# VectorE takes a slot's score maximum ahead of the q and k norm work in forgetting attention

## What is computed

```
q, k, v, g, f_logit = split(x @ w_in)              # 16 heads of 64
qh, kh = rms_norm(heads(q), qn_g), rms_norm(heads(k), kn_g)
c = cumsum(log_sigmoid(f_logit + b_f))             # per head, over time
s = (qh @ kh.T) / sqrt(64) + (c[t] - c[s]);  causal mask
o = softmax(s) @ vh;   o = o * sigmoid(g);   out = o @ w_out
```

## Time and profile before

| | us |
|---|---|
| median of 3 runs (1427.09 to 3438.35) | 1429.08 |
| profiled execution | 1426.63 |
| its span, first to last instruction | 1424.8 |
| TensorE busy | 1352.9 (95%) |
| VectorE busy | 506.6 (36%) |
| ScalarE busy | 492.9 (35%) |

### The profile page before, as it was taken

How to read it: one execution, slowest core, us unless ns; L and a number is a source line. 1 busy time by engine, 2 the same in 40 slices (tenths; PEclk the granted TensorE clock), 3 DMA queues, 4 the chain that set the end, 5 groups by cost and what they waited for, 6 DMA issues and landing times.

```text
span 1424.8 us, 19060 instructions
## 1 busy us (share of the span) xinstructions
PE 1352.9 (95%) x7304; PEld 1124.4 (79%) x7304; DVE 506.6 (36%) x1057; ACT 492.9 (35%) x830; POOL 530.3 (37%) x421
## 2 busy tenths in 40 slices
PE   7999997789999999999998999999999999999997
PEld 7887875568888888888887788777788888888886
DVE  3366435646111111010763766654571111110005
ACT  4312326533322332221254655554333232232111
POOL 5422222042454444544144222222244445445440
PEclk9999998999999999999999999999999999999999
DMA  6211120022333332323123122212223333333231
GB/s 222 99 57 60 60 89 30 30 79 70 89 89 93 114 89 93 122 96 105 60 60 106 45 61 60 60 35 85 67 82 89 111 96 89 94 99 118 89 104 59
DMA packets 140233, 119.61 MB, mean 84 GB/s; under 512 B 5648, under 2 KB 118512, under 8 KB 140144
## 3 DMA queue, kind: packets, MB, share of 16 engines
q1 hardware_dynamic: 140144, 118.41, 26.5%
HBM read 116.20 MB, written 2.10 MB: 83 GB/s over the span
## 4 chain that ended last, share of the span: by engine, by line
PE 79%; DVE 9%; ACT 5%; issue 4%; POOL 1%; DMA 0%; ACTq 0%; DVEq 0%; SPq 0%; POOLq 0%
PE banks L471 24%; PE banks L473 24%; PE banks L472 24%; ACT w_hi L1038 1%; PE banks L750 1%; PE banks L863 1%; POOL w_lo L998 1%; PE banks L897 1%; PE banks L879 1%; ACT p_fox L1295 1%; DVE fox_ms L1579 1%; PE banks L542 1%; DVE x_res L1532 1%; PE banks L768 1%; DVE small L1494 1%
## 5 line engine op out<-in xcount | busy, mean ns | idle before, releaser
L998 POOL TENSOR_TENSOR w_lo<-w_raw,w_hi 128x512 fp32r<-128x512 f32 x417 | 530.1, 1304 | 862.6 <-ACT w_hi L1038 848.6
L471 PE MATMUL banks<-xT_lo,w_hi 128*128 128x512 f32 (+2 forms) x992 | 370.6, 374 | 2.2 <-DVEq L1337 1.6
L473 PE MATMUL banks<-xT_hi,w_hi 128*128 128x512 f32 (+2 forms) x992 | 367.4, 370 | 0.0
L472 PE MATMUL banks<-xT_hi,w_lo 128*128 128x512 f32 (+2 forms) x992 | 367.4, 370 | 0.0
L1038 ACT ACTIVATE w_hi<-w_raw 128x2048 fp32r<-128x2048 f32 (+1 forms) x107 | 200.0, 1869 | 192.2 <-PE banks L473 150.9
L471 PEld LDWEIGHTS banks<-xT_lo,w_hi 128*128 128x128 f32 (+1 forms) x992 | 185.4, 187 | 36.1 <-issue 4.9
L473 PEld LDWEIGHTS banks<-xT_hi,w_hi 128*128 128x128 f32 (+1 forms) x992 | 185.3, 187 | 32.8
L472 PEld LDWEIGHTS banks<-xT_hi,w_lo 128*128 128x128 f32 (+1 forms) x992 | 185.5, 187 | 31.2
L471 PE MATMUL banks<-w_lo,xT_hi 128*128 128x256 f32 (+1 forms) x544 | 185.5, 341 | 10.0 <-ACT q_raw L1060 3.3
L472 PE MATMUL banks<-w_hi,xT_lo 128*128 128x256 f32 (+1 forms) x544 | 179.5, 330 | 0.0
L473 PE MATMUL banks<-w_hi,xT_hi 128*128 128x256 f32 (+1 forms) x544 | 179.4, 330 | 0.0
(11 more groups left out here) (179 smaller groups left out, 1231.2 us busy)
## 6 DMA issues: line engine op xcount, KB each, us to landing
w_raw<-in_ffn_w_dram SPq DMA_DIRECT2D x92, 512.0 KB, 4.5
w_raw<-in_ffn_w_dram SPq DMA_DIRECT2D x20, 1024.0 KB, 4.8
w_raw<-in_fox_w_in_dram SPq DMA_DIRECT2D x16, 1024.0 KB, 5.8
w_raw<-in_even_w_in_dram SPq DMA_DIRECT2D x14, 1024.0 KB, 4.9
w_raw<-in_even_w_out_dram SPq DMA_DIRECT2D x4, 1024.0 KB, 4.9
w_raw<-in_fox_w_out_dram SPq DMA_DIRECT2D x4, 1024.0 KB, 4.8
x_res<-in_x_dram SPq DMA_DIRECT2D x4, 512.0 KB, 7.5
out_dram<-x_res SPq DMA_DIRECT2D x4, 512.0 KB, 2.6
```

What stands on the lines that cost most here:

```text
L471: mm(acc, l_hi, r_lo, start=first, stop=False)
L472: mm(acc, l_lo, r_hi, start=False, stop=False)
L473: return mm(acc, l_hi, r_hi, start=False, stop=final)
L998: ins = nc.gpsimd.tensor_tensor(w_lo[c % RING][:, a:a + n], w_raw[c % RAW][:, a:a + n], w_hi[c % RING][:, a:a + n].bitcast(F32), ALU.subtract)
```

## The change

At each entry that has a slot, VectorE's maximum is issued first, ahead of `fox_heads` of i-2 and `square_sums` of i-1 (and of the forget gate's work, which lies at entries without slots). No operation is added or removed, and no other engine's list is touched.

```
             for i, (piece, s) in enumerate(fox_steps):
-                if heads_at(i - 2):
-                    fox_heads(*heads_at(i - 2))
-                if heads_at(i - 1):
-                    square_sums(*heads_at(i - 1))
-                if i == 2 * NT:
...
-                if i == 2 * NT + 1:
...
                 if s is not None and s < F_UNITS:
                     n = (s % NT + 1) * P
                     c = 2 * (s % 4)
...
                     chain(ins, S["fmax"])
+                if heads_at(i - 2):
+                    fox_heads(*heads_at(i - 2))
+                if heads_at(i - 1):
+                    square_sums(*heads_at(i - 1))
+                if i == 2 * NT:
...
+                if i == 2 * NT + 1:
...
                 if s is not None and 1 <= s <= F_UNITS:
```

More of the change, by code:

```diff
@@ L1605, in _ @@
             for i, (piece, s) in enumerate(fox_steps):
+                if s is not None and s < F_UNITS:
+                    n = (s % NT + 1) * P
+                    c = 2 * (s % 4)
+                    if s >= 4:
+                        dve.wait_ge(S["fexp"], s - 3)
+                    for m in range(2):
+                        full(("fs", s, m))
+                    a, b = SCORE_BANKS[s % 3]
+                    if b - a == 1:
+                        ins = v.tensor_reduce(small[:, 16 + c:18 + c], banks[:, a:b + 1, 0:n], AX_X, ALU.max,
+                                              negate=True)
+                    else:
+                        step(v.tensor_reduce(small[:, 16 + c:17 + c], psum[a][:, 0:n], AX_X, ALU.max, negate=True))
+                        ins = v.tensor_reduce(small[:, 17 + c:18 + c], psum[b][:, 0:n], AX_X, ALU.max, negate=True)
+                    chain(ins, S["fmax"])
                 if heads_at(i - 2):
@@ L1624, in _ @@
                     chain(v.tensor_copy(parts[2], z), S["c_split"])
[L1625 to L1639, removed]
                 if s is not None and 1 <= s <= F_UNITS:
```

## The result

The changed kernel took 1461.45 us (median of 4 runs, 1460.29 to 1462.64) against 1428.09 us: a ratio of 1.0236, 95% interval 1.0224 to 1.0249. It is slower by 33 us. One of the four executions of before took 3438.35 us, for a reason that no trace here shows; its other three took 1425.9 to 1429.08. The prediction was 1448 us with a range of 1433 to 1460, so the direction was right and the loss larger than the range allowed by 1.5 us. The profiled execution took 1462.64 us with a span of 1460.9.

A forecast was written before the change was run, and what follows sets the result against it. TensorE, busy 95% of the span, was taken as the bound. The profiled 1426.6 us plus 19.9 us of costed delays gave 1446.5, and one fall of the clock, 1.7 us, made 1448 us; range 1433 to 1460.

The forecast's parts named there:

- What it costs: Prediction's section pricing the later Exp in fourteen slots with norm work, less lateness saved and TensorE's slack: 19.9 us in total.
- The term for each slot: Exp later by 2.5 us, or 3.95 beside GpSimd, less saved lateness; after slack, 0.5 to 2.9 us reach TensorE.
- slots 6 and 14, and I cost nothing: Slots where only fox_heads of i-2 is moved and ScalarE has no root to wait for: costed at nothing.
- the cover: At slots 6 and 14 the heads' turn is a whole piece after fox_heads; failing, it costs 1.2 us each.
- I take one fall for the forecast: TensorE's clock falls once after a new long stall, losing 1.7 us.
- Rival 1: Clock falls behind every long stall, slots 2, 3, 5, 10, 11, 18, 20: 12 us on top, 1458 us; chance 0.16.
- ScalarE's wait: Sign: ScalarE's wait for square_sums, ahead of its root, should rise from 22.7 us to about 55.
- TensorE's three waits: Sign: waits for a piece's evacuation, prob_copy freeing bank 3 and Exp freeing a scores bank rise about 20 us together.
- The end of the stretch: Sign: the stretch from 770 us, where slots and q, k pieces stand together, should end near 955 instead of 935.
- Rivals 2: The earlier maximum counts: TensorE's waits for Exp and prob_copy go, 4.2 us, giving 1422; chance 0.05.
- 3 and 4: 3: TensorE's piece hides the late Exp, 1427 to 1433; 4: the change does nothing, 1427; chance together 0.14.
- the maximum's lateness: Before, VectorE still at the norms started the maximum late, up to 2.0 us per slot; 11.7 us saved in all.

The follow-up runs named there:

- e10: Changed kernel with ScalarE's turned_heads ahead of the weight rounding at slots 6, 14, 21 and spare matmuls in TensorE's stalls behind slots 1, 3, 11, 19: 1451.69 us.
- e1: Changed kernel with ScalarE's root of a piece moved behind the Exp and prob_copy of the same entry; VectorE's order stays changed: 1436.29 us.
- e2: Changed kernel with square_sums moved back ahead of the maximum, fox_heads staying behind it: 1432.83 us.
- e3: Changed kernel with fox_heads moved back ahead of the maximum, square_sums staying behind it: 1440.59 us.
- e7: Changed kernel with ScalarE's turned_heads ahead of the weight chunk's rounding at the entries of slots 6, 14 and 21: 1452.95 us.
- e6: Changed kernel with spare matmuls, read by nobody, at ten places in TensorE's stalls: 1455.98 us.
- e9: Kernel of before, with VectorE's order square_sums, maximum, fox_heads at slots 1, 2, 4, 9, 10, 17 and 19 only: 1427.57 us against 1428.51.

## Why the prediction was right, and where it failed

Each line is how much longer the way from one score to the next became, by slot, in us:

```
slot                     1    2    3    4    5    6    9   10   11   12   13   14   17   18   19   20   21    sum
costed, "What it costs" 0.5  2.3  2.8  0.9  0.8  0    0.5  2.0  2.9  0.5  1.0  0    0.5  2.5  1.0  1.7  0    19.9
changed kernel          0.4  2.1  3.8  1.3  0.8  1.7  0.4  1.8  3.3  2.8  1.0  2.8  0.4  2.3  2.7  1.8  2.2  31.8
e10                     0.4  2.1  3.2  0.9  0.8  1.4  0.4  1.8  3.3  0.4  1.0  1.2  0.5  3.8  1.1  1.8 -0.7  23.3
```

**The mechanism** was right. The Exp stands behind the root, the root behind `square_sums`, and this behind the maximum. e1 takes that link out and the loss goes; e2 and e3 show that it is `square_sums` that starts it and `fox_heads` that lengthens it.

**The term for each slot** was right where nothing was missing: in e10, eleven of the fourteen slots with norm work lie within 0.2 us of what was costed. Slots 3 and 11 are 0.4 above it, since `fox_heads` beside GpSimd took 3.25 us (800.72 to 803.97 at slot 3) and not 2.7; slot 18 holds the one fall of the clock that is left there.

The measured 31.8 us are 11.9 more than the 19.9 that I had costed. Of these, 6.7 lie at slots 6, 14 and 21, which I had at nothing; 1.4 at slots 3 and 4, 2.7 at 11 and 12 and 1.5 at 18 and 19, with the falls of the clock in them; the other slots are about 0.5 below.

**The first step that failed is "slots 6 and 14, and I cost nothing".** Slot 21 belonged in that list too, and it is missing there. I looked at VectorE and not at what stands in ScalarE's list between the late Exp and the next use of bank 3. The rounding, 1.91 us, had lost its cover. Three waits behind it took 1.45, 1.45 and 1.22 us, and 3.2 us of the clock loss came with them. What I had named as the cover, a whole piece between `fox_heads` and its turn, held in the changed kernel; with the copy moved ahead (e7, e10) it failed by 0.6 us at each of the two slots, since `fox_heads` took 4.4 us there beside GpSimd and not 1.25.

**The second, and by the numbers the larger, is "I take one fall for the forecast".** There were six stretches at the low clock, with a clock loss of 12.7 us, where I had put 1.7; I had named more than two falls as a sign that the forecast is wrong. Rival 1, which priced a fall for each long stall at 1458 us, came within 4 us of the result, in part by luck: of its seven slots the clock fell at 2, 3 and 11, and the falls at 14, 19 and 21 are not in its list, nor are the waits behind the rounding. I gave it 0.16 on the ground that the slow stretch covers part of the next wait. That ground holds, for up to more than half of the clock loss that e6 took away, but the falls were so many that the rest still counted. The rival's condition, a stall between 1.24 and 2.40 us, doesn't hold as it stands: the clock fell behind slot 2's stall of 1.65 us and stayed at 1.00 behind e2's of 2.41 us. How long the one stall is doesn't decide alone, and what does isn't shown here. The Trainium skill's rule ("TensorE: Matmul & The Clock Gate", section "Why this matters for your kernels") is that idle gaps between bursts of matmuls bring the clock back to half rate, but the gaps that it warns of are longer than the 1.7 to 2.9 us of rival 1, so it did not speak for that rival. It agrees with this trace at slot 3, where TensorE stalled 3.77 us and the stretch from 806 to 813 us is at 0.52; the fall behind slot 2, after 1.65 us, goes beyond it, and there the measurement decides.

The sum by experiments closes too: 19.9 us as costed, 6.4 by e7, 2.0 by the fillers on top of it, and 3.5 that stay in e10 beyond the costed terms: 2.6 at slots 6 and 14 (0.6 us of late evacuation and 0.6 of late turn at each are its waits), 1.7 us of clock loss at slot 18, less 0.8 elsewhere; together 31.8. What the falls alone cost in time isn't settled, because a slow stretch and a wait overlap. A small part of the miss is the base: the 19.9 us were added to the profiled execution, 2.5 us under the median that I had; from the median the forecast would have been 1451 us.

Of the signs that I named, the maximum starts 0.42 us after the scores' last matmul (I said 0.44), ScalarE's wait is 57.9 us (I said about 55), and TensorE's three waits rose by 16 us, not 20; at slot 2 the slow stretch had taken the place of such a wait. The end of the stretch moved by more than the 20 us that I gave: the scores of slot 21 came 29.6 us later than before, counted from slot 0.

Rivals 2, 3 and 4 are out. What of the maximum's lateness was won is at most about 1 us of the stage (e9), not 4.2, and no difference in the time: the rest came back as a wait for late `fox_heads` in e2, and for the copy of turned heads in e9 (TensorE's wait for it is 4.5 us there, 1.8 before).

## What to carry to other kernels

When an instruction is moved ahead on one in-order engine, read the list of the engine that consumes it: an earlier result is worth nothing if something else that now comes later stands ahead of its consumer. Then follow the delayed consumer to everything queued behind it, housekeeping such as a weight rounding included, for it has lost its cover too. And where the sum yields many stalls of TensorE about as long as one that already cost a fall of the clock, several falls belong in the range, less what the next wait would have taken anyway; which of the stalls will bring one could not be told here from their length.

## What the hardware showed

The clock can fall after a stall shorter than the 2.40 us that I had as the nearest row: ahead of slot 2's scores TensorE had stalled 1.65 us, and the stretch behind them was at 0.57. It need not fall after a longer one: in e2 it stayed at 1.00 behind a stall of 2.41 us, and in e10 no fall followed stalls of 1.93 us (slot 2) and 1.62 us (slot 20). A low clock is not always lost time: behind slot 2 the slow piece stood where e6, at the full clock, waited 1.94 us; the way to the next scores was 2.1 us longer than before in both. Beside GpSimd, the same five small VectorE operations (`fox_heads`) took 3.25 us at slot 3 and 4.4 us at slot 6 of e10, against 1.25 without it.
